# TensorE's share of each expert value row as four 64x64 tiles, VectorE's half of the sum in SBUF, and score products of two head halves side by side

## The reference, cut to what matters

```python
# PEER: 16 experts for each of 8 heads, so 128 expert rows for each token
ue = jnp.take(expert_u, expert, axis=0)
ve = jnp.take(expert_v, expert, axis=0)
h = jax.nn.gelu(jnp.einsum('thkd,td->thk', ue, xc), approximate=False)
return jnp.einsum('thk,thkd->td', gate * h, ve)
...
# differential attention: c is one of two halves (64 wide) of a head
s = jnp.einsum('bqhcd,bkhcd->bhcqk', q_blk, k) * scale
s = jnp.where(causal_mask(i, S)[None, None, None], s, -jnp.inf)
```

## Time and profile before

| | |
|---|---|
| median of 3 runs | 3069.66 us (3062.38 to 3070.73) |
| profiled execution | 3067.13 us, of which 3065.2 us are the span from first to last instruction |
| mean granted TensorE clock | 0.934 |
| PE / DVE / ACT / POOL busy | 2637.0 / 1926.5 / 1410.8 / 1648.5 us |
| rows alone | 620 to 1235 us |
| rows beside half 0 | 1235 to 2322 us |
| half 1 alone | 2322 us to the end |

### The profile page before, as it was taken

The page is one execution under the profiler, slowest core; times in us unless marked ns, Lnnn a source line. Parts: engine busy times, 40 slices in busy tenths (PEclk is TensorE's granted clock), DMA queues, the critical chain, the costliest instruction groups (busy, mean ns, idle before and its releaser), DMA issues.

```text
span 3065.2 us, 46495 instructions
## 1 busy us (share of the span) xinstructions
PE 2637.0 (86%) x17182; PEld 2006.6 (65%) x17182; DVE 1926.5 (63%) x4115; ACT 1410.8 (46%) x3130; POOL 1648.5 (54%) x973
## 2 busy tenths in 40 slices
PE   6987977988887777698899987679997999999998
PEld 3865965743333333276478876458886979998998
DVE  5676443767777777776876668677666463256323
ACT  2231122243344343456865556775554454545543
POOL 3822113734444443465278866357883618863785
PEclk8998978999999999898899998899997999999999
DMA  7210013279999999779779997989995405542453
GB/s 293 99 58 26 4 56 151 105 314 421 422 421 421 421 421 412 317 291 394 277 304 408 406 365 302 360 315 389 409 412 210 145 17 188 175 145 76 152 187 116
DMA packets 140529, 797.42 MB, mean 260 GB/s; under 512 B 15504, under 2 KB 18704, under 8 KB 67600
## 3 DMA queue, kind: packets, MB, share of 16 engines
q0 software_dynamic: 73728, 536.90, 43.1%
q1 hardware_dynamic: 65856, 253.09, 23.1%
q10 hardware_dynamic: 720, 4.46, 0.3%
HBM read 787.84 MB, written 6.55 MB: 259 GB/s over the span
## 4 chain that ended last, share of the span: by engine, by line
PE 44%; DVE 15%; DMA 15%; issue 8%; POOL 7%; ACT 6%; DVEq 0%; ACTq 0%; SPq 0%; POOLq 0%
PE ps L2503 9%; PE ps L2522 8%; PE ps L1742 7%; PE ps L1948 5%; DMA raw<-in_peer_uv,un 5%; PE ps L872 4%; DVE scratch L1848 3%; POOL wls L303 3%; PE ps L333 3%; DMA un<-in_peer_uv,un 2%; DMA w<-in_peer_uv,scratch 2%; POOL wlw L303 1%; DMA raw<-in_peer_uv,scratch 1%; DMA w<-in_peer_uv,un 1%; DVE ts L2043 1%
## 5 line engine op out<-in xcount | busy, mean ns | idle before, releaser
L303 POOL TENSOR_TENSOR wls<-raws,whs 128x1024 fp32r<-128x1024 f32 (+1 forms) x256 | 612.4, 2402 | 376.6 <-ACT whs L297 371.4
L1742 PE MATMUL ps<-raw,un 128*128 128x512 f32 x522 | 278.2, 641 | 71.8 <-ACT un L1804 70.7
L1948 PE MATMUL ps<-ts,whs 128*128 128x256 f32 x1424 | 300.7, 312 | 27.5 <-DVE ts L2043 19.7
L1723 POOL DMA_INDIRECT raw<-in_peer_uv,un x205 | 205.6, 1003 | 205.1 <-PE ps L1742 130.1
L297 ACT CAST whs<-raws 128x1024 fp32r<-128x1024 f32 (+1 forms) x256 | 263.7, 1036 | 92.3 <-PE ps L2522 33.7
L303 POOL TENSOR_TENSOR wlw<-raws,whw 128x1024 fp32r<-128x1024 f32 x112 | 267.8, 2405 | 69.8 <-ACT whw L297 69.0
L1948 PEld LDWEIGHTS ps<-ts,whs 128*128 128x128 f32 x1424 | 238.9, 202 | 59.5 <-issue 33.5
L1797 ACT ACTIVATE un<-un 128x1 f32<-128x1 f32 x384 | 77.6, 202 | 431.8 <-DVE scratch L1848 422.6
L2522 PE MATMUL ps<-ts,whs 128*128 128x256 f32 x1216 | 240.1, 299 | 0.0
L1848 DVE SCALAR_TENSOR_TENSOR scratch<-raw,ps 128x1024 f32<-128x1024 f32 x149 | 181.4, 1217 | 93.2 <-DMA raw<-in_peer_uv,un 86.8
L2503 PE MATMUL ps<-ts,whs 128*128 128x256 f32 x1088 | 209.9, 294 | 0.0
(11 more groups left out here) (437 smaller groups left out, 7073.6 us busy)
## 6 DMA issues: line engine op xcount, KB each, us to landing
raws<-in_w_up SPq DMA_DIRECT2D x128, 512.0 KB
raws<-in_w_down SPq DMA_DIRECT2D x128, 512.0 KB
scratch<-in_ada_w SPq DMA_DIRECT2D x17, 1024.0 KB, 13.5
raws<-in_w_qk SPq DMA_DIRECT2D x32, 512.0 KB
raw<-in_w_in SPq DMA_DIRECT2D x11, 1024.0 KB, 5.4
raw<-in_peer_w_q SPq DMA_DIRECT2D x8, 1024.0 KB, 7.9
raws<-in_w_v SPq DMA_DIRECT2D x16, 512.0 KB
raws<-in_w_o_a SPq DMA_DIRECT2D x16, 512.0 KB
```

What stands on the lines that cost most here:

```text
L303: e.tensor_tensor(self.wl[h][:, 0:width], self.raw[slot][:, 0:width], self.wh[h][:, 0:width].bitcast(F32), ALU.subtract).then_inc(*self.ti ...
L1723: e.indirect_dma_start(self.rows[r], None, self.d["peer_uv"], index).then_inc(*self.tick(f"row{r}", n, 16))
L1742: ins = e.matmul(self.ps[:, b + half, :], self.diag[n >= 128][n % 4], self.rows[self.row_of(n)][:, 1024 + 512 * half:1536 + 512 * half], s ...
L1948: ins = e.matmul(o[:, 0:256], l, r, start=k == 0 and i == 0, stop=k == nk - 1 and i == 2)
```

## The change

Each value row now goes through the array as four 64x64 tiles. The constant `iota` gets, in its columns 64 to 127, a one where column and partition agree modulo 64, and a diagonal matrix becomes 128x64: its upper 64 partitions are the diagonal block of tokens 0 to 63, its lower ones that of tokens 64 to 127. `hd` picks the token half (array rows, and its own PSUM bank), `half` the column half (array columns, and PSUM partitions 0 to 63 or 64 to 127). In the joint part a tile has 256 columns, before it 512. VectorE's half of the sum moves from PSUM bank 7, which TensorE's second token half now takes, into SBUF (`vacc`). `act_join`, `pe_join` and `dve_join` follow the new places. In `scores` the products of c = 0 and c = 1 stand next to each other, and both PSUM banks are waited for before the first. The numbers of steps, and so the interleaving, stay as they are.

```diff
-    m = {"ident": r == c, "ones": np.ones((128, 128)), "bd": same, "iota": np.broadcast_to(c, (128, 128)),
+    m = {"ident": r == c, "ones": np.ones((128, 128)), "bd": same, "iota": np.where(c < 64, c, r % 64 == c % 64),
...
+        self.diag = [[s[:, 256 + 64 * i:320 + 64 * i] for i in range(4)] for s in small]
+        self.vacc = small[1][:, 512:1024]
+        self.each64 = self.C("iota")[:, 64:128]
...
-                for half in range(1 if self.both_add(n) else 2):
-                    ins = e.matmul(self.ps[:, b + half, :], self.diag[n >= 128][n % 4],
-                                   self.rows[self.row_of(n)][:, 1024 + 512 * half:1536 + 512 * half], start=k == 0,
-                                   stop=k == 127)
+                row, diag = self.rows[self.row_of(n)], self.diag[n >= 128][n % 4]
+                w = 256 if self.both_add(n) else 512
+                for half in range(2):
+                    for hd in range(2):
+                        p, o, a = slice(64 * hd, 64 * hd + 64), slice(64 * half, 64 * half + 64), 1024 + w * half
+                        ins = e.matmul(self.ps[o, b + hd, 0:w], diag[p, :], row[p, a:a + w], start=k == 0, stop=k == 127)
...
-        e.activation(self.diag[n >= 128][n % 4], self.C("ident"), ACT.Identity, bias=0.0,
+        e.activation(self.diag[n >= 128][n % 4], self.each64, ACT.Identity, bias=0.0,
...
+        e.copy(sums[:, 0:512].rearrange("p (b n) -> p b n", b=2), self.ps[:, b:b + 2, 0:256]).then_inc(*self.tick("peer_act"))
+        e.wait_ge(*self.at("peer_dve", ("acc", 128 * tt + 127)))
+        e.copy(sums[:, 512:1024], self.vacc).then_inc(*self.tick("peer_act", ("sums", tt)))
...
+    def dve_add(self, e, n):
+        S, acc = "peer_dve", self.vacc
...
+            e.scalar_tensor_tensor(out=acc, in0=v, scalar=w, in1=acc, op0=ALU.mult, op1=ALU.add).then_inc(*self.tick(S, ("acc", n)))
...
+            outs = []
             for c in range(2):
...
+                outs.append((o, slice(64 * c, 64 * c + 64)))
...
+                for o, p in outs:
                     e.matmul(o[:, 0:256], H.q[p, hh, qs], self.kA[p, hh, :], start=True, stop=True)
+            for o, p in outs:
                 e.matmul(o[:, own:w], H.q[p, hh, qs], H.k[p, hh, 0:w - own], start=True, stop=False)
+            for c, (o, p) in enumerate(outs):
                 e.matmul(o[:, 128 * qb:w], self.C("ident"), self.C("causal"), start=False,
                          stop=True).then_inc(*self.tick(S, ("score", n, c)))
```

More of the change, by code:

```diff
@@ L1366, in peer_tiles @@
         small = (self.junk[1], un[:, 5120:6144])
-        self.dots, self.gelus, self.weight = ([s[:, 128 * i:128 * i + 128] for s in small] for i in range(3))
-        self.diag = [[s[:, 512 + 128 * i:640 + 128 * i] for i in range(4)] for s in small]
+        self.dots, self.weight = ([s[:, 128 * i:128 * i + 128] for s in small] for i in range(2))
+        self.diag = [[s[:, 256 + 64 * i:320 + 64 * i] for i in range(4)] for s in small]
+        self.vacc = small[1][:, 512:1024]
+        self.each64 = self.C("iota")[:, 64:128]
     @staticmethod
@@ L1755, in pe_join @@
         for half in range(2):
-            tile, freed = ("join", tt, half), ("join_dve", ("x", tt, 4 * half + 3))
+            tile, freed = ("join", tt, half), ("join_dve", ("x", tt, 4 * half + 3 if tt >= 2 else 5 + 2 * half))
             o, before = self.slot(tile, freed)
@@ L1760, in pe_join @@
             for k in range(4):
-                c = 512 * half + 128 * k
+                c = 512 * half + 128 * k if tt >= 2 else 512 * (k % 2) + 128 * (2 * half + k // 2)
                 ins = e.transpose(o[:, 128 * k:128 * k + 128], self.sums[tt % 2][:, c:c + 128], self.C("ident"))
@@ L1820, in dve_rows @@
             if 0 <= n < 512 and self.both_add(n):
[L1821 to L1824, removed]
-                    e.tensor_scalar(acc, v, w, None, ALU.mult).then_inc(*self.tick(S, ("acc", n)))
-                else:
-                    e.wait_ge(*self.at(S, ("acc", n - 1)))
-                    e.scalar_tensor_tensor(out=acc, in0=v, scalar=w, in1=acc, op0=ALU.mult,
-                                           op1=ALU.add).then_inc(*self.tick(S, ("acc", n)))
+                self.dve_add(e, n)
             if n in (130, 386 + LAG):
@@ L1833, in dve_rows @@
             yield
+    def dve_add(self, e, n):
+        S, acc = "peer_dve", self.vacc
+        v, w = self.rows[self.row_of(n)][:, 1536:2048], self.weight[1][:, n % 128:n % 128 + 1]
+        e.wait_ge(*self.at("peer_act", ("weight", n)))
+        if n % 128 == 0:
+            e.wait_ge(*self.at("peer_act", ("sums", n // 128 - 1)))
+            e.tensor_scalar(acc, v, w, None, ALU.mult).then_inc(*self.tick(S, ("acc", n)))
+        else:
+            e.wait_ge(*self.at(S, ("acc", n - 1)))
+            e.scalar_tensor_tensor(out=acc, in0=v, scalar=w, in1=acc, op0=ALU.mult, op1=ALU.add).then_inc(*self.tick(S, ("acc", n)))
     def dve_dot(self, e, n):
@@ L1852, in dve_join @@
     def dve_join(self, e, tt, j):
-        ts = slice(128 * tt, 128 * tt + 128)
-        e.wait_ge(*self.at("peer_pe", ("join", tt, j // 4)))
-        e.scalar_tensor_tensor(out=self.xT[:, j, ts], in0=self.bh(("join", tt, j // 4), 512)[:, 128 * (j % 4):128 * (j % 4) + 128],
-                               scalar=self.modv[:, 40 + j:41 + j], in1=self.xT[:, j, ts], op0=ALU.mult,
+        x, gain = self.xT[:, j, 128 * tt:128 * tt + 128], self.modv[:, 40 + j:41 + j]
+        if tt >= 2 and j >= 4:
+            tile = ("join", tt, 1)
+            turned = self.bh(tile, 512)[:, 128 * (j - 4):128 * (j - 4) + 128]
+        elif tt >= 2:
+            tile = ("join", tt, 0)
+            turned = self.bh(tile, 512).rearrange("p (d k s n) -> p k s d n", d=2, k=2, n=64)[:, j % 2, j // 2]
+            x = x.rearrange("p (d n) -> p d n", n=64)
+        else:
+            tile = ("join", tt, j % 4 // 2)
+            turned = self.bh(tile, 512).rearrange("p (k s d n) -> p k s d n", s=2, d=2, n=64)[:, j % 2, :, j // 4]
+            x = x.rearrange("p (s n) -> p s n", n=64)
+        e.wait_ge(*self.at("peer_pe", tile))
+        e.scalar_tensor_tensor(out=x, in0=turned, scalar=gain, in1=x, op0=ALU.mult,
                                op1=ALU.add).then_inc(*self.tick("join_dve", ("x", tt, j)))
```

21 lines of the change are left out of this document (11 added, 10 removed).

## The result

The changed kernel takes 3109.72 us (median of 4 runs, 3102.22 to 3113.32), against 3066.76 us (median of 4) for the kernel before beside it: ratio 1.0137, 95% interval 1.0112 to 1.0162. It is slower by 1.4%, some 43 us, where I had forecast 3062. Its page begins as follows, to be read against the earlier trace rows.

A forecast was written before the change was run, and what follows sets the result against it. Gathers bound the rows alone, TensorE, DMA and POOL together the MLP stretches, TensorE half 1's attention. Terms -5 - 6 - 2 + 18 - 10 - 2 = -7 us gave 3062, range 3038 to 3121.

The forecast's parts named there:

- Rows alone, 0: Before 1235 us: gathers bound this part, so halving TensorE's work at best changes the time by 0.
- A visit, 0.84 us: A joint value row on TensorE: 0.43 us with four tiles at once plus 0.41 round trip, against 0.86 before.
- column tiles in turn: Rival, chance 0.20: column tiles on one row group take turns, a visit costs 0.2 or 0.4 us more; 3080 or 3121.
- strict order: Rival, chance 0.04: TensorE keeps program order, a visit is five units of 0.213 plus 0.41 us; 3164.
- Joint tiles, -5 - 6 - 2 = -13: Joint part: 5 us from directly following rows, 6 from visits at half clock, 2 from ScalarE's shorter diagonal.
- Scores, -10 and -2: Paired score products: 10 us gained in half 1 (ends 5 and 15), 2 in half 0 (ends -2 and 5).
- VectorE's add in SBUF, +18: MLP stretches: longer L303 beside adds make 56 us on POOL, a third on the path; ends 0 and 56.
- the lock decides: Rival, chance 0.18: add and POOL block each other in the MLP stretches, costing all 56 us, not 18; 3100.
- The new add's tail: Sign in the profile after: the new add (L1846) has a median near 0.75 us and a tail to 3 us.
- The lock costs nothing: Rival, chance 0.17: idle time of POOL and VectorE in the MLP stretches absorbs the add's blocking; -25, 3045.
- nothing moves: Rival, chance 0.04: gathers hide the row part and VectorE the scores; 3067 to 3071.
- Sum: All terms together: -5 - 6 - 2 + 18 - 10 - 2 = -7 us, rounded to 3062.

The follow-up runs named there:

- a plain delay of VectorE: Kernel before plus one VectorE multiplication by 1.0 in PSUM ahead of each joint add: 3104.15 us, ratio 1.0111.
- the narrow one: Add of 256 columns in SBUF: changed kernel with TensorE's part of a joint row widened to 768 columns; 3083.85 us, ratio 1.0054.

## Why the prediction was wrong, step by step

- **Rows alone, 0**: right. 1.0003.
- **A visit, 0.84 us**: nearly right, 0.79. Four tiles do run at once, so the rivals of column tiles in turn (0.20) and of strict order (0.04) fall. The Trainium skill, "TensorE: Matmul & The Clock Gate", Part 3, says that matmuls start and end strictly in program order. As I read it, with each tile's second record holding back the tiles behind it, it would make five units of 0.213 here, 1.07, and the trace disagrees with 0.66. The four first records begin within 21 ns and the four second ones 0.27 us later; in which order the program has the eight the trace doesn't say, so it refutes my reading and not surely the rule. The prices that the two rivals had outside the MLPs do not agree with their own words: half of 160 rows gives 32 and 50 us where I wrote 38 and 60.
- **Joint tiles, -5 - 6 - 2 = -13**: too much. Worth 1.5 us under the lock, within the noise; 10 us by medians with the add in PSUM and three banks. How much they give without a lock and with four banks stays open, since no bank is free for it.
- **Scores, -10 and -2**: right, -12 in the run of pairs alone.
- **VectorE's add in SBUF, +18**: this is the step that failed. It measured 58 (1.0189). That the add and L303 exclude each other was right, and VectorE's added time within a third (126 us; its busy time grew by 168). But the 18 is a third of 56 us on POOL alone, for all 186 L303 of the joint part. VectorE's 126 us got no term and no reason for having none. It is their price that was missing: a plain delay of VectorE costs 36 us, of which 30 outside the MLPs, where it is 73 us more busy, and 3 inside, where it is 88 us more busy. The add in SBUF lost 34 us outside (32 and 33 in the changed kernel), and 18 to 26 inside, near the 18. I had read from the earlier trace rows that the chain through gather, VectorE and ScalarE is late between the MLPs, and then left it out of the sum. The growth of these waits from 50 to 82 is not the measure of that: they are 62 with the add in SBUF alone and 51 with VectorE's delay, and of the 82 only 30 lie in the two stretches outside the MLPs (25 before). The measure is the chain of waits, in which VectorE's row steps between the MLPs go from 40 to 72 us.
- **The rival "the lock decides"** (0.18, 3100, place: POOL in the MLP stretches) came nearest in time, which is in part luck: its place accounts for less than half of the loss. Its 56 us on POOL by longer L303 did not come: L303 went from 2.40 to between 2.41 and 2.45 us, and the gather issues took 29 us more in its stead. The new add's tail went to 4.67 us, not to 3. *The lock costs nothing* (0.17) and *nothing moves* (0.04) fall with the same runs.
- **Sum**: 58 - 12 - 2 = 44 from the parts measured alone, against 43 measured, and 46 when the changed kernel was run again. Nothing is left over that these runs could show.

The Trainium skill, "SBUF — State Buffer", section "SBUF: two separate sides", has the two instructions exclude each other whole. The trace agrees, but for some 0.2 us: adds of 0.75 take 2.71 and 4.43 and end 0.56 us behind the last L303.

## What to carry to other kernels

Before a sum moves from PSUM to SBUF, look at what GpSimd does in the same stretch: here the add paid the rest of each GpSimd subtraction that it met, and every instruction queued behind it paid too. Price an added delay in each stretch by what is late there, and not only where the busy shares are highest; an engine that is idle for a quarter of the time can be the late one, as VectorE was between the MLPs. A delay of the suspected length, put on one engine in memory that nobody shares, tells in one run what a lateness costs. Don't take the count of one wait for its price: VectorE's delay cost 36 us and left TensorE's 50 waits for the diagonal at 51.

## What the runs showed of the hardware that was not expected

- Four 64x64 fp32 tiles on four quarters of the array, each of two records of 256 columns, run in 0.66 us together, and a visit of them between 128-row matmuls costs 0.79 us (0.86 for one product of 512 columns on the whole array).
- A gather issue is held up by a VectorE add too, but only by a long one: 1.22 us where an add of 0.75 us ends 0.40 us after the issue begins, 0.96 where one of 0.47 ends 0.14 us after it begins.
- Two L303 back to back leave a waiting add no gap: it waited for both (4.43 us; the longest was 4.67, and 5.61 for the narrow one).
- The tiles lower TensorE's granted clock where it waits much (0.77 against 0.93 at 1000 to 1050 us, 0.78 against 0.89 between the MLPs), and hardly in the MLP stretches (0.97 and 0.98 against 0.98 and 0.99). No time hung on it: 1.0003 with tiles in the rows-alone part only, and 3110.34 against 3111.84 us with and without them in the changed kernel.
- One PSUM bank less for half 0's tail (three in place of four) cost 29 us in this kernel.
